# GpSimd selections in place of TensorE mask products on the diagonal steps of a stick-breaking attention

## The reference, cut to what matters

```python
z = einsum("bqhd,bkhd->bhqk", qb, kb) * scale
strict = s_pos < t_pos
log_keep = where(strict, log_sigmoid(-z), 0.0)
after = cumsum(log_keep, reverse=True) - log_keep
weights = where(strict, exp(log_sigmoid(z) + after), 0.0)
out = einsum("bhqk,bkhd->bqhd", weights, vb)
```

## Time and profile before

| what | value |
|---|---|
| median of 3 runs | 2698.07 us (2697.26 to 2701.66) |
| the profiled execution, its own time | 2698.06 us |
| its span in the trace | 2696.3 us |
| TensorE matmul busy | 2546.7 us (94%) |
| VectorE busy | 1685.9 us (63%) |
| GpSimd busy | 1553.6 us (58%) |
| ScalarE busy | 1346.9 us (50%) |

### The profile page before, as it was taken

The page is one execution under the profiler, slowest core; times in us unless marked ns, Lnnn a source line. Parts: engine busy times, 40 slices in busy tenths (PEclk is TensorE's granted clock), DMA queues, the critical chain, the costliest instruction groups (busy, mean ns, idle before and its releaser), DMA issues. The chain is left out here.

```text
span 2696.3 us, 41194 instructions
## 1 busy us (share of the span) xinstructions
PE 2546.7 (94%) x14100; PEld 1797.1 (67%) x14100; DVE 1685.9 (63%) x2063; ACT 1346.9 (50%) x2095; POOL 1553.6 (58%) x1257
## 2 busy tenths in 40 slices
PE   4999999998999999889799999999999999599998
PEld 3788777776888888756555555555555555488887
DVE  5532555735214445257588889888888988655554
ACT  4433333344333333344377778777777877322221
POOL 5876666688777777568665666566566655000000
PEclk7999999998999999989889999999999999799999
DMA  2543323233433333257721130312212011423230
GB/s 105 156 137 124 127 96 121 104 102 125 133 117 121 118 133 121 72 144 189 199 75 59 53 95 25 95 56 64 75 43 88 29 44 52 158 91 113 79 113 35
DMA packets 204100, 268.74 MB, mean 100 GB/s; under 512 B 13440, under 2 KB 137664, under 8 KB 197264
## 3 DMA queue, kind: packets, MB, share of 16 engines
q1 hardware_dynamic: 203920, 266.43, 30.8%
HBM read 169.36 MB, written 97.03 MB: 99 GB/s over the span
## 5 line engine op out<-in xcount | busy, mean ns | idle before, releaser
L2040 POOL TENSOR_TENSOR a_w<-a_beta,a_rest 128x1024 f32<-128x1024 f32 (+2 forms) x320 | 560.4, 1751 | 354.9 <-DVE a_rest L1997 208.8
L764 POOL TENSOR_TENSOR f_l_lo<-f_wst,f_l_hi 128x512 fp32r<-128x512 f32 x312 | 405.4, 1303 | 269.4 <-ACT f_l_hi L632 269.1
L1997 DVE TENSOR_TENSOR_SCAN a_rest<-a_keep,a_rest,a_ones 128x513 f32<-128x513 f32 x384 | 470.1, 1262 | 10.8 <-ACT a_keep L1967 10.8
L1917 PE MATMUL a_turn<-a_ident,a_w 128*128 128x128 f32 (+1 forms) x2432 | 343.7, 279 | 7.2 <-DVE a_wt L1951 6.1
L1932 PE MATMUL a_o<-a_wt,a_v 128*64 128x512 f32 (+3 forms) x1408 | 339.4, 560 | 8.9 <-DVE a_out L2007 8.9
L500 PE MATMUL f_xz<-f_t_hi,f_l_hi 128*128 128x512 f32 x832 | 329.6, 396 | 6.9 <-issue 4.4
L1951 ACT COPY a_wt<-a_turn 128x512 f32<-128x512 f32 (+3 forms) x440 | 225.1, 528 | 207.8 <-PE a_turn L1917 206.3
L500 PE MATMUL f_xz<-f_t_hi,f_l_lo 128*128 128x512 f32 x832 | 325.7, 391 | 0.0
L500 PE MATMUL f_xz<-f_t_lo,f_l_hi 128*128 128x512 f32 x832 | 325.4, 391 | 0.0
L1917 PEld LDWEIGHTS a_turn<-a_ident,a_w 128*128 128x128 f32 (+1 forms) x2432 | 257.4, 140 | 91.4 <-issue 65.8
L1967 ACT ACTIVATE a_keep<-a_z 128x1024 f32<-128x1024 f32 (+4 forms) x352 | 300.0, 852 | 4.5 <-PE a_z L1900 4.5
(11 more groups left out here) (251 smaller groups left out, 4270.1 us busy)
## 6 DMA issues: line engine op xcount, KB each, us to landing
f_wst<-in_w_pairs SPq DMA_DIRECT2D x52, 1024.0 KB, 5.8
scratch_gate<-f_out SPq DMA_DIRECT2D x64, 256.0 KB, 2.3
o_g<-scratch_mixed SPq DMA_DIRECT2D x32, 512.0 KB, 5.5
scratch_xbc<-f_out SPq DMA_DIRECT2D x36, 256.0 KB, 2.1
scratch_q_hi<-f_out SPq DMA_DIRECT2D x32, 256.0 KB, 3.1
scratch_q_lo<-f_out SPq DMA_DIRECT2D x32, 256.0 KB, 3.5
scratch_v<-f_out SPq DMA_DIRECT2D x32, 256.0 KB, 2.3
s_xc<-scratch_xbc SPq DMA_DIRECT2D x16, 512.0 KB, 5.6
```

The lines of the kernel that those rows point to most:

```text
L764: return nc.gpsimd.tensor_tensor(out, a, b, op).then_inc(done, 1)
L1917: mm = nc.tensor.transpose(turn[h][0:rows, qi * P:(qi + 1) * P], tile[:, h, x:x + rows], ident[:, :])
L1997: mm = nc.vector.tensor_tensor_scan(rest[r % RS][:, h, tn - 1::-1], top, ones[:, 0:1].to_broadcast([P, tn]), start, ALU.mult, ALU.min)
L2040: nc.gpsimd.tensor_tensor(w[r % AS][:, :, 0:tn], beta[r % KEEPS][:, :, 0:tn], rest[r % RS][:, :, 1:tn + 1], ALU.mult).then_inc(w_ready, 1)
```

## The change

TensorE's two mask products of each diagonal step go away, and so do the two bf16 constants. GpSimd gets two `affine_select` instructions for each diagonal step, one on keep (fill 1) and one on beta (fill 0). Each covers both heads and only the columns of the query block's own keys (2 x 128, 2 x 112 in block 3, 2 x 16 in the tail), and works in place. VectorE's scan waits for the masked keep, GpSimd's weigh for the masked beta. GpSimd's order becomes, for each n: mask beta of n (if diagonal), mask keep of n+1 (if diagonal), weigh(n).

```diff
     def constants(self, pool):
-        for tile in (self.ident, self.ident16, self.never):
-            nc.gpsimd.memset(tile[:, :], 0.0).then_inc(self.zeroed, 1)
...
+        nc.gpsimd.memset(self.ident[:, :], 0.0).then_inc(self.zeroed, 1)
+        pool.wait_ge(self.zeroed, 1)
...
+    MASKS = [sum(diagonal(x) for x in range(n)) for n in range(N + 1)]
+
+    def own_keys(n):
+
+        _, _, qi = unit(n)
+        if qi is None:
+            return W + 1, META, P - META
+        first = META + qi * P
+        return first, width(n) - first, 0
...
-                if diagonal(n):
-                    for h in range(2):
-                        if qi is None:
-                            z_part, never_part = z[n % 2][:, h, 0:META], never[:, P - META:P]
-                        else:
-                            z_part = z[n % 2][:, h, META + qb * P:tn]
-                            never_part = never[:, 0:tn - META - qb * P]
-                        mm = nc.tensor.matmul(z_part, ident16[:, :], never_part, start=False, stop=True,
-                                              skip_group_check=True)
                 mm.then_inc(z_ready, 1)
...
-                dve.wait_ge(keep_ready, START + n + 1)
+                if diagonal(n):
+                    dve.wait_ge(keep_masked, START + MASKS[n + 1])
+                else:
+                    dve.wait_ge(keep_ready, START + n + 1)
...
+            def mask(tile, n, fill, done):
+                at, count, skipped = own_keys(n)
+                part = tile[side(n) % KEEPS][:, :, at:at + count]
+                nc.gpsimd.affine_select(out=part, in_=part, compare_op=ALU.is_gt, fill=fill, base=-skipped,
+                                        pattern=[[0, 2], [-1, count]], channel_multiplier=1).then_inc(done, 1)
+
+            def mask_keep(n):
+                pool.wait_ge(keep_ready, START + n + 1)
+                mask(keep, n, 1.0, keep_masked)
+
+            def mask_beta(n):
+                pool.wait_ge(beta_ready, START + n + 1)
+                mask(beta, n, 0.0, beta_masked)
+
             def weigh(n):
...
                 pool.wait_ge(beta_ready, START + n + 1)
+                if diagonal(n):
+                    pool.wait_ge(beta_masked, START + MASKS[n + 1])
...
+            mask_keep(0)
             for n in range(N):
+                if diagonal(n):
+                    mask_beta(n)
+                if n + 1 < N and diagonal(n + 1):
+                    mask_keep(n + 1)
                 if not is_tail(n):
                     weigh(n)
```

More of the change, by code:

```diff
@@ L1667, in __init__ @@
         self.ident = self.sbuf("a_ident", [P, P])
-        self.ident16 = self.sbuf("a_ident16", [P, P], BF16)
-        self.never = self.sbuf("a_never", [P, P], BF16)
         self.zeroed, self.made = self.sem("a_zeroed"), self.sem("a_made")
@@ L1709, in constants @@
         nc = self.nc
-        for tile in (self.ident, self.ident16, self.never):
-            nc.gpsimd.memset(tile[:, :], 0.0).then_inc(self.zeroed, 1)
[L1712 to L1716, removed]
+        nc.gpsimd.memset(self.ident[:, :], 0.0).then_inc(self.zeroed, 1)
+        pool.wait_ge(self.zeroed, 1)
+        nc.gpsimd.affine_select(out=self.ident[:, :], in_=self.ident[:, :], compare_op=ALU.not_equal, fill=1.0, base=0,
                                 pattern=[[-1, P]], channel_multiplier=1).then_inc(self.made, 1)
@@ L1813, in attention_stage @@
         k_high, k_low, q_high, q_low, v, gate = early.k_high, early.k_low, early.q_high, early.q_low, early.v, early.gate
-        ident, ident16, never = early.ident, early.ident16, early.never
+        ident = early.ident
         keep, beta = ring("keep", KEEPS, (P, 2, SIDE)), ring("beta", KEEPS, (P, 2, SIDE))
@@ L1830, in attention_stage @@
         scanned, w_ready, padded = m_.sem("scanned"), m_.sem("w_ready"), m_.sem("padded")
+        keep_masked, beta_masked = m_.sem("keep_masked"), m_.sem("beta_masked")
         turned = m_.sems("a_turned", 2)
@@ L1935, in apply @@
                 mm.then_inc(applied, 1)
-            pe.wait_ge(made, START + 3)
+            pe.wait_ge(made, START + 1)
             for n in range(-2, N + LAG + 1):
```

## The result

| what | kernel before | changed kernel |
|---|---|---|
| median | 2696.45 us (2693.05 to 2701.66, 14 runs) | 2702.16 us (2699.89 to 2705.48, 14 runs) |
| the profiled execution, its own time | 2698.06 us | 2700.05 us |
| its span in the trace | 2696.3 us | 2698.3 us |

The changed kernel takes 1.002 of the time of the kernel before [1.0012, 1.0029], 5.7 us more. The forecast was 5.4 us more, with 2698.07 for the kernel before. More runs put that at 2696.45, so the forecast of 2703.5 is 1.3 us above the median and inside its range.

The account below looks back on a forecast made before the run. TensorE and VectorE were taken to bound the path alternately, about half the rounds each. Per pair -0.67 + 0.96 + 0.08 + 0.3 = +0.67 us, +5.4 in all on 2698.06, gave 2703.5 us, range 2687 to 2720.

Parts of the forecast that it names:

- 0.3 of idle latencies: Masks on GpSimd that wait for keep (steps 4, 9, 31) start late: 0.15 us twice on the path per pair.
- What TensorE gives up: Mask products dropped from TensorE's diagonal steps: 17 us ceiling, 1.64 us a pair where TensorE sets the time, 13.1 in all.
- What a selection costs: On GpSimd, 0.40 us for 2 x 128 columns, the next starting 0.36 after; bounds 0.29 and 0.57.
- The walk of the third chunk: Places 13 to 20: scans wait for mask_keep behind weigh on GpSimd, scan 18 1.5 us late, 0.96 us lost per pair.
- Some 13 or 14 selections per pair: Selections lying on the path where scans wait for masks, 108 in all; used for the bounds 2691.5 and 2722.
- What would show it: Signs: scans 1, 6, 15, 16, 18, 28 released by GpSimd; TensorE waiting for copies in rounds 2, 17, 29; pair near 117.8 us.
- That the gain gets through: Rival: gaps at the diagonals take in the masks, 13.1 us gained, 2685 us; decided by mask_keep(18) ending before 1737.8; chance 0.20.
- its partial form: Milder form of the gain getting through: only the third chunk's 0.96 and 0.41 stay, about 2693 us.
- That they cancel: Rival: same mechanism a little cheaper, no 0.3 of latencies, a few hits taken in; 2692.7 to 2703.4, about 2700; chance 0.28.
- Stretched selections: Rival: VectorE working beside GpSimd stretches a selection to 0.54 us, 15 us on top, 2718.6 us; chance 0.12.
- 12 cycles per element: Skill's rule for data-dependent branching on GpSimd, 2.6 us for 256 columns; the prediction said this selection doesn't branch.

Follow-up runs that it names:

- The work without the waits: Changed kernel with all 320 selections made on spare tiles that nobody waits for, so the diagonal stays unmasked: 2687.85 us.
- no masks: Changed kernel with the selections and their waits removed, so nothing masks the diagonal steps: 2686.78 us.
- Two ahead: Changed kernel with the mask of keep n+2 issued first in round n, ahead of beta n and weigh(n): 2690.16 us.
- keep ahead of beta: Changed kernel with only the order of the two masks swapped, mask_keep(n+1) ahead of mask_beta(n): 2699.64 us.
- both kernels with masks two ahead: Changed kernel with mask_keep two steps ahead everywhere, 2690.16 us, or only at steps 1, 2, 6, 7, 15, 16, 18, 28, 29, 2691.34 us.
- both masks: Changed kernel with TensorE's mask products and their constants put back beside GpSimd's selections: 2706.54 us.
- keep alone: Changed kernel without the selections on beta, those on keep and their waits staying: 2694.71 us.
- products in the third chunk: Changed kernel with the third chunk's diagonal (steps 14 to 18) masked by TensorE's products again, the other three by selections: 2696.05 us.
- twice and two ahead: Changed kernel with mask_keep two steps ahead and every selection doubled by one into a spare tile: 2718.34 us.
- each selection twice: Changed kernel with a second selection of the same size, into a spare tile, ahead of each of the 320: 2753.65 us.

## Why the prediction was right, and what in it was not

The changed kernel is slower for the reason given: the mask of keep stands behind weigh on GpSimd, VectorE's scans wait for it, and the copies behind them come late to TensorE. The work without the waits (1.1 us) and the same work in another order (12 us less) show that it is the place and not the work. The sum's size owes something to chance, since two of its terms were too large and of opposite sign (1.64 and 2.31 us a pair, measured 1.06 and 1.64). By stretches of a pair, from the timelines in us (changes worked out from the medians of the pairs; "gain" is no masks against before, "loss" the changed kernel against no masks):

| stretch | gain forecast | gain measured | loss forecast | loss measured | net forecast | net measured |
|---|---|---|---|---|---|---|
| first and second chunk (43 to 14) | 0.94 | 0.68 | 0.27 + 0.2 | 0.24 | -0.47 | -0.44 |
| third chunk (14 to 28) | 0.41 | 0.27 | 1.37 | 1.18 | +0.96 | +0.91 |
| fourth chunk (28 to 43) | 0.29 | 0.11 | 0.37 + 0.1 | 0.24 | +0.18 | +0.13 |
| a pair | 1.64 | 1.06 | 2.31 | 1.64 | +0.67 | +0.58 |

The last row is the median of whole pairs, so it isn't quite the sum of those above. The 0.3 of idle latencies is split there as its three steps lie, two in the first part. Times 8 the net is 4.7 us by the traces (4.3 with the mean of the changed kernel's pairs, 117.66) and 5.7 by the medians. The difference isn't placed.

- **"What TensorE gives up": too large.** The place of the gain was right. The step that failed is the price of a product, taken as the distance to the next start. The transposes behind it take 0.05 longer without it, so 13.1 us became 8.4 by the traces and 9.9 by the medians.
- **What a selection costs: right.** 0.40 forecast, 0.412 measured, the next 0.36 after it in both.
- **The walk of the third chunk: right to 0.02 us.** Counted from the end of scan 13 (1730.48 in the walk, 1730.65 in the trace): scan 16 starts 4.57 later by the walk and 4.59 in the trace (1735.24), the second half of round 17's transposes 5.78 and 5.80, scan 18 8.87 and 8.88, the copy of round 20 15.34 and 15.32. The 0.05 taken for the signal to the scan was close: the mask of keep 18 ends at 1739.50 and the scan starts at 1739.53.
- **The idle latencies of 0.3: not on the path.** They exist: a mask that waits for keep starts some 0.14 us after it. But in the first two chunks the whole loss is 0.24, less than the 0.27 without them.
- **"Some 13 or 14 selections per pair": too few.** The doubled selections show 16 (by pairs) to 18 (by medians). That count entered only the range.
- **What would show it.** The six scans named are released by GpSimd (steps 0, 4, 9 and 31 too). In the pair shown TensorE's weight loads wait for the copy in rounds 17 and 29, as forecast, but in round 7 and not in round 2. Scan 18 starts 1.24 us after the transposes of its round (1738.30) where it started 0.05 before them, so 1.3 later against them, forecast about 1.5. A pair takes 117.70, forecast 117.8.

**The rivals.** That the gain gets through fell for this order: the mask of keep 18 ends at 1739.50, long past the 1737.8 at which that rival decided. Two ahead is that rival made true by moving one call, though 2690 is nearer to its partial form than to the full 2685. That they cancel, "about 2700", isn't refuted by the time alone: 2702.16 lies in its range of 2692.7 to 2703.4, and its "no 0.3 of latencies" is what the traces show. Against the median of before as it came out, the loss of 5.7 us is just over the 5.3 that this range allowed. Stretched selections fell: 0.412 us beside VectorE's scans, not 0.54, and the products of 1024 columns take 2.00 us in the mean before and after. As the prediction read the Trainium skill ("GPSIMD Engine Reference", section 8, Key points), a scan with one input in PSUM shouldn't contend, and these durations agree. The 12 cycles per element of the Trainium skill's section 3.1 on that page don't show in this selection: 2.6 us by an estimate from them, 0.412 in the trace.

## What to carry to other kernels

An instruction added to an in-order engine costs by its place in the order: here the same 320 selections cost 1.1 us when nobody waited for them, 3.4 when those of keep were issued two steps ahead, and 15.4 when many stood behind a product of up to 2 us (by the medians; by undisturbed pairs 0.0, 0.07 and 1.60 us a pair). Before moving work to an engine with free time, look for what stands ahead of it, and put it where that engine waits anyway. What a removed instruction gives back is read from the start of the work before it to the end of the work behind it, since the next one may take longer without it. And where two orders differ by a few us, look at the clock of each trace by pair, or whatever repeats, before the difference is put down to the order.

## What the runs showed of the hardware

**The clock of TensorE falls after short waits, in some pairs.** In the kernel with keep ahead of beta, one pair took 118.31 us where its neighbours took 117.03. Its windows (us, busy us of PE, PEld, DVE, ACT, POOL; clock; DMA):

```profile
1605.00:1610.50 5.50, 4.56 (x36) 2.88 (x36) 5.50 (x6) 5.50 (x10) 4.03 (x3) 1.00 0.04 12
1610.50:1614.50 4.00, 3.62 (x14) 1.80 (x15) 3.63 (x5) 0.09 (x1) 2.81 (x3) 0.57 0.60 180
1614.50:1620.00 5.50, 5.50 (x40) 2.64 (x38) 3.22 (x6) 3.91 (x10) 4.54 (x9) 1.00 0.21 60
```

And TensorE's timeline there:

```profile
1609.11 0.66 PE L1913 MATMUL a_turn<-a_ident,a_w 128*128 128x128 f32 x4 [0.21 <-DVE a_wt L1947]
...
1610.88 1.84 PE L1928 MATMUL a_o<-a_wt,a_v 128*64 128x512 f32 x4 [1.11 <-DVE a_out L2006]
...
1614.82 1.08 PE L1928 MATMUL a_o<-a_wt,a_v 128*64 128x512 f32 x4
```

After waits of 0.21 and then 1.11 us the granted clock is 0.57 for 4 us, most of it at the lower of the two levels (1.2 GHz), and four products of the apply take 1.84 us in place of 1.08. The pair loses 1.3 us. The same 1.11 us wait stands in the other pairs and kernels (at 1727.73 in the changed one) mostly without such a fall. What decides between them stays open.

It is no small part of the experiments' times. Over the attention the traces of the changed kernel, no masks, the unawaited work and both kernels with masks two ahead have no such stretch. The kernel before has one (its last pair, 118.63 us in place of 117.12), both masks one, keep alone two, keep ahead of beta and products in the third chunk three each, twice and two ahead seven, and each selection twice eight. What one costs depends on who sets the time behind it: 0.8 us in both masks, 1.3 in keep alone, 1.5 in the third chunk's products and in twice and two ahead. In each selection twice a short one costs nothing in the end. TensorE waits for VectorE's copies afterwards, and by round 26 the pairs are level again at 123.6; only the two pairs with a longer one are 0.7 and 0.9 us late.

**A wait that the profile puts down to nothing can be an ordinary one.** The changed kernel's waits over the attention have this row, which the kernel before has not:

```profile
POOL a_w L2055 <- issue: 30.5, 15, 2.3
```

All 15 are weighs of steps 9 and 31, and each starts 0.22 us after the end of its own scan. The scan of step 9 in the pair shown (the second head's) and its weigh:

```profile
1717.89 1.24 DVE L1996 TENSOR_TENSOR_SCAN a_rest<-a_keep,a_ones 128x529 f32<-128x529 f32 x1
1719.36 2.06 POOL L2055 TENSOR_TENSOR a_w<-a_beta,a_rest 128x1058 f32<-128x1058 f32 x1 [2.29 <-issue]
```

The scan ends at 1719.13. So these are waits for late scans that the profile failed to name, and no idle time of another kind.

**Every second pair is 0.15 us longer.** In every second pair of the changed kernel the weigh of step 4 starts 0.51 us after its scan's end and not 0.23, and the pairs alternate between some 117.72 and 117.57 us. Keep ahead of beta has the same 0.51; both masks and products in the third chunk, with the same selections on GpSimd in the first chunk, have 0.22 or 0.23 in every pair after the first. What causes it stays open.

**Medians and traces part by a few microseconds.** No masks and two ahead have nearly the same span in the trace (2686.4 and 2686.8), yet their medians are 2686.78 and 2690.16. The profiled execution is 1.3 us above the median of its kernel in the first and 1.6 below it in the second. With one trace for each kernel, that difference can't be placed.
